# Expert stage of a one-layer MoE trunk: pairs of experts in 64 slots with two gate/up passes, down projection in float32 on raw weights

## The reference

```python
g_val, g_idx = lax.top_k(group_prob, 1)
e_val, e_idx = lax.top_k(in_group, TOP_K_IN_GROUP)            # 2 of the 8 experts of the group
e_w = jax.nn.softmax(e_val, axis=-1) * g_val
for grp in range(N_GROUPS):                                   # 4 groups of 8 experts
    hid = (jax.nn.silu(jnp.einsum('nd,edf->nef', t, w_e_gate[sl]))      # 2048 -> 256
           * jnp.einsum('nd,edf->nef', t, w_e_up[sl]))
    out = out + jnp.einsum('nef,efd->nd', hid * combine[:, sl, None], w_e_down[sl])   # 256 -> 2048
```

## Time and profile before

| | us |
|---|---|
| median of 3 runs | 1174.81 |
| the runs | 1174.03, 1174.81, 6625.89 |
| span of the profiled execution | 1173.3 |

### The profile page before, as it was taken

The page is one execution under the profiler, slowest core; times in us unless marked ns, Lnnn a source line. Parts: engine busy times, 40 slices in busy tenths (PEclk is TensorE's granted clock), DMA queues, the critical chain, the costliest instruction groups (busy, mean ns, idle before and its releaser), DMA issues.

```text
span 1173.3 us, 15718 instructions
## 1 busy us (share of the span) xinstructions
PE 1148.3 (98%) x5398; PEld 952.8 (81%) x5398; DVE 827.2 (70%) x741; ACT 675.1 (58%) x610; POOL 19.5 (2%) x21
## 2 busy tenths in 40 slices
PE   7999999999999999999999999999999999999995
PEld 6888888888888888878878888888888888888884
DVE  5546565565554545654578887988879888798887
ACT  5335555643333344443567776677766777667774
POOL 0000000000000000111100000000000000000000
PEclk8999999999999999999999999999999999999998
DMA  9554444577566565585659998999989999799991
GB/s 314 189 188 162 153 162 174 173 244 271 194 201 211 190 209 177 199 285 178 215 180 333 382 374 306 313 375 379 373 299 319 371 385 373 291 325 368 378 354 74
DMA packets 115094, 312.05 MB, mean 266 GB/s; under 512 B 14152, under 2 KB 15216, under 8 KB 114544
## 3 DMA queue, kind: packets, MB, share of 16 engines
q1 hardware_dynamic: 115056, 311.55, 74.7%
HBM read 309.41 MB, written 2.10 MB: 265 GB/s over the span
## 4 chain that ended last, share of the span: by engine, by line
PE 90%; DVE 5%; ACT 3%; issue 2%; DMA 0%; DVEq 0%; SPq 0%; ACTq 0%
PE bank L1392 28%; PE bank L1394 27%; PE bank L1393 27%; PE bank L1699 2%; ACT whi L528 1%; DVE wlo L1238 1%; DVE o_lo L1278 1%; PE bank L1494 1%; DVE wlo L849 1%; PE bank L1518 1%; PE bank L1686 1%; PE bank L1596 0%; DMA x<-in_x 0%; DVE y_out L1366 0%; DVE xs L873 0%
## 5 line engine op out<-in xcount | busy, mean ns | idle before, releaser
L1238 DVE TENSOR_TENSOR wlo<-xraw,whi 128x2048 fp32r<-128x2048 f32 x186 | 425.1, 2291 | 71.3 <-ACT whi L528 70.2
L528 ACT ACTIVATE whi<-xraw 128x2048 fp32r<-128x2048 f32 x188 | 360.7, 1919 | 94.8 <-PE bank L1394 93.2
L849 DVE TENSOR_TENSOR wlo<-raw,whi 128x2048 fp32r<-128x2048 f32 x92 | 214.8, 2336 | 209.2 <-ACT whi L528 209.2
L528 ACT ACTIVATE whi<-raw 128x2048 fp32r<-128x2048 f32 x92 | 176.2, 1916 | 255.0 <-PE bank L1394 255.0
L1392 PE MATMUL bank<-whi,actT_hi 128*128 128x512 f32 x608 | 240.6, 396 | 4.9 <-DVE actT_lo L880 2.1
L1394 PE MATMUL bank<-wlo,actT_hi 128*128 128x512 f32 x608 | 237.6, 391 | 0.0
L1393 PE MATMUL bank<-whi,actT_lo 128*128 128x512 f32 x608 | 237.4, 390 | 0.0
L1392 PE MATMUL bank<-whi,xg_hi 128*128 128x512 f32 x512 | 202.0, 394 | 0.3 <-DVE wlo L1238 0.3
L1394 PE MATMUL bank<-wlo,xg_hi 128*128 128x512 f32 x512 | 199.6, 390 | 0.0
L1393 PE MATMUL bank<-whi,xg_lo 128*128 128x512 f32 x512 | 199.5, 390 | 0.0
L1392 PEld LDWEIGHTS bank<-whi,actT_hi 128*128 128x128 f32 x608 | 114.6, 188 | 31.4 <-DVE wlo L849 3.7
(11 more groups left out here) (216 smaller groups left out, 861.6 us busy)
## 6 DMA issues: line engine op xcount, KB each, us to landing
xraw<-in_w_e_gate SPq DMA_DIRECT2D x126, 512.0 KB, 5.0
xraw<-in_w_e_up SPq DMA_DIRECT2D x126, 512.0 KB, 6.5
xraw<-in_w_e_down SPq DMA_DIRECT2D x124, 512.0 KB, 6.1
raw<-in_w_gate SPq DMA_DIRECT2D x64, 512.0 KB, 4.3
raw<-in_w_in SPq DMA_DIRECT2D x56, 512.0 KB, 4.6
raw<-in_w_out SPq DMA_DIRECT2D x32, 512.0 KB, 4.8
raw<-in_w_branch_a SPq DMA_DIRECT2D x16, 512.0 KB, 4.7
raw<-in_w_branch_b SPq DMA_DIRECT2D x16, 512.0 KB, 4.7
```

The lines of the kernel that those rows point to most:

```text
L528: return act.activation(whi[slot][:], src, ACT.Copy)
L849: dve.tensor_tensor(wlo[s][:], raw[:, k, :], whi[s][:], ALU.subtract).then_inc(lo_made, 1)
L1238: dve.tensor_tensor(wlo[s][:], place(i, j, q)[0], whi[s][:], ALU.subtract).then_inc(lo_made, 1)
```

## The change

1. **Slots by pair.** A group's 8 experts form 4 pairs. A token is given a slot in each pair in which it has an expert, 64 slots (`CAP`) a pair. `selp` holds these 0/1 matrices. `gather` now multiplies the fp32r parts `hg_hi` and `hg_lo` by the four pairs at once (256 columns) and leaves both parts beside each other in `xe`: 64 slots of high part and 64 of low part form the 128 stationary columns of gate/up.
2. **Gate/up in two passes.** PE multiplies the stacked columns by `whi` and by `wlo`: rows 0 to 63 of the result hold the high part's product, rows 64 to 127 the low part's. ACT copies the lower gate rows (`gate_low`), DVE adds them (`gate_sum`), ACT runs silu for both row halves, and the matmul that turns the hidden rows has the 0/1 matrix `p2` in place of the identity: it adds the two halves and puts each row at its slot among the group's 128.
3. **Down in float32.** `hT_e` is kept in float32, and `down` multiplies it by the loaded weights as they are: no `whi`/`wlo`, one float32 matmul for each 512 columns. There are two `whi`/`wlo` pairs now.
4. **Loads.** Down row blocks come in one DMA of 1 MiB. The order in the queue becomes gate/up 0, 1, down block 0 of the expert before, gate/up 2, 3, down block 1. A place with a down block is free when PE has used it (`after_down`). Before the first group 8 pieces are loaded instead of 10.
5. **Routing.** The counts run over 20 columns (4 groups and 16 pairs) in place of 4, `hg` is made in two parts on DVE (`gained`) instead of on POOL, and tokens for which a pair or group has no room go through all 32 experts in float32, under an `If`.

From the diff, cut to what is spoken of:

```diff
+        def gate_up_at(j, k4):
+            return 2 + k4 if j == 0 else (0, 1, 3, 4)[k4]
+        def down_at(j, f):
+            return (j + 1, (2, 5)[f]) if j + 1 < EPG else (EPG, f)
...
+                if j == 0:
+                    after_down(i - 1, EPG - 2, 0)
+                    load_gate_up(i, 0, 0, e)
+                    after_lo(i - 1, EPG - 1, 2)
+                    load_gate_up(i, 0, 1, e)
+                    after_lo(i - 1, EPG - 1, 3)
+                    load_gate_up(i, 0, 2, e)
+                    after_down(i - 1, EPG - 2, 1)
+                    load_gate_up(i, 0, 3, e)
+                elif j == 1:
+                    if not first:
+                        after_down(i - 1, EPG - 1, 0)
+                        load_gate_up(i, 1, 0, e)
+                        after_down(i - 1, EPG - 1, 1)
+                        load_gate_up(i, 1, 1, e)
+                        after_lo(i, 0, 0)
+                        load_down(i, 0, 0, e)
...
-            pool.wait_ge(g2_in, 16)
-            with pool.Fori(0, NC) as n:
-                for t in range(TT):
...
+            def gained(n):
+                steps = Chain(dve, hg_step, 4 * n)
+                for t in range(TT):
+                    dve.wait_ge(acc_free, 2 * (A1 + A2 + NC) + 2 + 2 * n + t + 1)
+                    cols = bass.ds(n * COLS, COLS)
+                    dve.wait_ge(hg_made, 2 * n + t + 1)
+                    steps.link(dve.tensor_tensor(hgt[:], resid[:, t, cols], gbig[:, cols], ALU.mult))
+                    steps.link(dve.tensor_copy(permuted(hg_hi[t][:], n), by_rows(hgt[:])))
+                    dve.tensor_tensor(permuted(hg_lo[t][:], n), by_rows(hgt[:]), permuted(hg_hi[t][:], n),
+                                      ALU.subtract).then_inc(hg_made, 1)
...
+            def group_v(i, after_another, another_follows):   # DVE
+                if after_another:
+                    output_lo(i - 1)
+                for j in range(EPG):
+                    expert_lo(i, j, 2)
+                    if j == 0:
+                        weights(i)
+                    expert_lo(i, j, 3)
+                    if j == 0 and after_another:
+                        add(i - 1, range(0, 6), SCATTER)
+                    if j < EPG - 1:
+                        expert_lo(i, j + 1, 0)
+                        gate_sum(i, j)
+                        expert_lo(i, j + 1, 1)
+                        hidden(i, j)
+                    if j == 0 and after_another:
+                        add(i - 1, range(6, 8), SCATTER)
...
+            def gate_up(i, j, k4):
+                    for part in (whi, wlo):
+                        mm = pe.matmul(dst[:], x, part[s][:].rearrange("p (u k f) -> p u k f", u=2, k=4)[:, :, k, :],
+                                       start=(kt == 0 and part is whi), stop=(kt == KT - 1 and part is wlo))
...
+            def down(i, j, f, blocks):
+                for b in blocks:
+                    mm = pe.matmul(bank[2 + b][:], hT_e[:, f, :], src[:, b * COLS:(b + 1) * COLS],
+                                   start=(j == 0 and f == 0), stop=last)
...
+            def gather(i, kts):
+                for kt in kts:
+                    if kt > 1:
+                        pe.wait_ge(xe_by_dve if kt % 2 else xe_by_act, KT // 2 * i + kt // 2)
+                    for h, part in enumerate((hg_hi, hg_lo)):
+                        for t in range(TT):
+                            mm = pe.matmul(bank[6 + kt % 2][:, h * 256:(h + 1) * 256], part[t][:, kt * P:(kt + 1) * P],
+                                           selp[:, t, 0:NP, :].rearrange("p r s -> p (r s)"),
...
+                for j in range(1, EPG):                       # PE, one expert
+                    gate_up(i, j, 0)
+                    down(i, j - 2, 1, (2, 3))
+                    turn_hidden(i, j - 1)
+                    gate_up(i, j, 1)
+                    down(i, j - 1, 0, (0, 1))
+                    gate_up(i, j, 2)
+                    down(i, j - 1, 0, (2, 3))
+                    gate_up(i, j, 3)
+                    down(i, j - 1, 1, (0, 1))
+                last = EPG - 1                                # PE, the seam
+                    gather(i + 1, range(0, 2))
+                down(i, last - 1, 1, (2, 3))
+                    gather(i + 1, range(2, 4))
+                turn_hidden(i, last)
+                    gather(i + 1, range(4, 7))
+                down(i, last, 0, (0, 1))
+                    gather(i + 1, range(7, 10))
+                down(i, last, 0, (2, 3))
+                    gather(i + 1, range(10, 13))
+                down(i, last, 1, (0, 1))
+                    gather(i + 1, range(13, 16))
+                down(i, last, 1, (2, 3))
```

More of the change, by code:

```diff
@@ L40 @@
 DENSE_RAW, DENSE_PARTS = 4, 2
-EXP_RAW, EXP_PARTS = 6, 3
+ROW = 6
+CAP = 64
 LOWEST = -3.0e38
@@ new lines, in gate_low, with silu @@
+            def gate_low(i, j):
+                act.wait_ge(gu_used, hi_count(i, j, 3) + 1)
+                act.activation(g_low[:], bank[j % 2][CAP:P, 0:FF], ACT.Copy).then_inc(g_low_made, 1)
+            def silu(i, j):
+                act.wait_ge(cw_made, 3 * i + 3)
+                act.wait_ge(g_sum_made, EPG * i + j + 1)
+                for h in range(2):
+                    rows = slice(h * CAP, (h + 1) * CAP)
+                    act.activation(s_act[rows, :], g_sum[:], ACT.Silu,
+                                   scale=cw[0:CAP, j // 2, EPG:EPG + 1]).then_inc(silu_made, 1)
@@ L820, in _ @@
+            bring_table(ACT.Silu)
+            for kt in range(0, KT, 2):
+                gathered_a(0, kt)
             group_a(0, False, True)
@@ new lines, in _ @@
+            dve.wait_ge(rank_full, 2)
+            for t in range(TT):
+                order.mark(dve.scalar_tensor_tensor(out=pos[:, t, :], in0=bank[2 + t][:, 0:NM], scalar=1.0,
+                                                    in1=member[:, t, :], op0=ALU.add, op1=ALU.mult))
+            order.wait()
+            for t in range(TT):
+                order.mark(dve.tensor_tensor(over[:, t, :], pos[:, t, :], room_of[:], ALU.subtract))
+            order.wait()
+            order.link(dve.tensor_reduce(worst[:], over[:], AX_X, ALU.max))
@@ L1215, in _ @@
+            gathered_v(0, 1)
+            dve.tensor_scalar(left[:], kept[:], -1.0, 1.0, ALU.mult, ALU.add).then_inc(left_made, 1)
             dve.wait_ge(gexp_made, TT)
@@ new lines, in group_v @@
+                if another_follows:
+                    expert_lo(i + 1, 0, 0)
+                gate_sum(i, EPG - 1)
+                if another_follows:
+                    gathered_v(i + 1, 1)
+                hidden(i, EPG - 1)
+                if another_follows:
+                    gathered_v(i + 1, 3)
+                    expert_lo(i + 1, 0, 1)
+                    for kt in range(5, KT, 2):
+                        gathered_v(i + 1, kt)
+                else:
+                    output_lo(i)
@@ L1665, in down @@
-            def down(i, j, start, stop):
-                pe.wait_ge(hT_lo_made, EPG * i + j)
-                for f in range(2):
-                    m = 6 * j + 2 + f
-                    q = 4 + f if not stop else f
-                    if stop:
-                        m = 6 * j - 2 + f
-                    s = (4 + q) % EXP_PARTS
-                    pe.wait_ge(lo_made, DENSE_RAW + DENSE + PER_G * i + m + 1)
-                    for b in range(4):
-                        cols = slice(b * COLS, (b + 1) * COLS)
-                        mm = three(bank[2 + b][:], hT_hi[:, f, :], hT_lo[:, f, :], whi[s][:, cols], wlo[s][:, cols],
-                                   start and f == 0, stop and f == 1)
-                        if stop and f == 1 and b < 3:
-                            mm.then_inc(o_full, 1)
-                    mm.then_inc(piece_used, 1)
+            pe.wait_ge(e_lo, 1)
```

801 lines of the change are left out of this document (417 added, 384 removed).

## The result

The changed kernel takes **1262.5 us** (median of 4 runs, 1261.4 to 1263.7) against 1174.8 for the kernel before: ratio 1.075, 95% interval 1.074 to 1.076. It is slower, and outside the range that was predicted (1160 to 1218). One run of the kernel before took 6625.9 us; it stands outside the comparison, and its cause is not known. The profiled execution has a span of 1260.5 us, 71.3 more than the 1189.2 of my sum. The direction came as forecast: the loads took over from PE. The size did not, and what sets their pace is not what I had priced.

A forecast was written before the change was run, and what follows sets the result against it. PE paced the kernel before; the load queue was to take over. The first group's last gate/up at 716.7, three periods of 147.7 and the tail gave 1189.2, with 1.5 for the median 1191 us; range 1160 to 1218.

The forecast's parts named there:

- my sum: Whole kernel: the forecast's terms added up to a span of 1189.2 us, against 1173.3 before.
- The ring's length: Inside a group, from one landing of gate/up piece 0 through PE's down half to the next: 15.65 us, pace taken 15.5.
- 0.2 + 2.5 + 5.1: Inside a group, from the down block's release to the next piece 0's landing: hand-over 0.2, fixed 2.5, transfers 5.1 us.
- the runs of loads: Inside groups, 30 pieces and then three times 33, up to the last gate/up's end: 86.2 us and 94.0 us each.
- The queue stays at its 40 us rate: Rival, loads inside groups: 2.75 us a piece, 16.5 an expert, total 1212 us; chance 0.24.
- bounds of the pace are 15.36 and 15.65: Inside a group, time per expert: between the queue's 15.36 us and the walked 15.65; 15.5 taken.
- The loads keep PE's pace: Rival, loads inside groups: 14.7 us an expert, needing 428 GB/s, total 1174 us; chance 0.17.
- PE's terms: PE's work per expert: 14.70 us against 16.58, with float32 matmuls of 512 columns at 0.875 and the turn at 0.45.
- The seam: Between two groups, from the old group's last gate/up to the next group's first down block done: 53.7 us.
- Routing: Before the first group: gather starts at 588.2 and takes 10.2 us, first gate/up at 598.4, 10.8 later than before.
- up to 4 us: In the routing, idle PE falling to the lower clock slows the 24 idle matmuls: up to 4 us more, not summed.
- The sign of the whole: Whole kernel: slower by 15.9 us, the saving per expert being spent at the seam, three times.

The follow-up runs named there:

- experiment 1: Changed kernel with SP's load list reordered, each down block asked for one gate/up piece later except a group's last: 1203.6 us.
- experiment 5: Changed kernel with the down blocks asked for by POOL on a DMA queue of their own, gate/up loads in their old order on SP: 1208.1 us.
- experiment 3: Changed kernel with only the second down block (f = 1) of each expert asked for later, f = 0 left in place: 1258.4 us.
- experiment 9: Kernel with reordered list, moved rounding and moved additions (1177.7 us), loading only 1 KiB of each 8 KiB row in all down blocks but the first: 1163.2 us.
- version two: Kernel with reordered list, moved rounding and moved additions (1177.7 us), last gained rows after the second last logits, 36 idle matmuls for 24: 1174.5 us.

## Why the prediction was wrong

**The ring's length: the step that failed.** I walked the right ring, "The next piece 0 so lands at t+7.85+0.2+2.5+5.1 = t+15.65", and made 15.5 an expert of it. The turn shown above takes 17.8. The term that was mis-sized is 0.2 + 2.5 + 5.1 = 7.8 us from the release of the down block to the landing: it measures 9.5 in that turn (650.78 to 660.28), 10.2 in the turn of the timelines (838.88 to 849.08), and 8.3 to 10.8, on the mean 9.5, in the 21 such waits that the chain shows. The 2.5 + 5.1 is the landing in an empty queue. I had only one ring in mind; the block f = 0 with pieces 2 and 3 makes a second one, half an expert away, whose last piece is still in the queue: in the timelines it is taken at 842.79, 3.7 us after the bunch of f = 1 was asked for. A small term was low too: gate/up 2.08 and not 1.81. This step holds most of the 58 us that the runs of loads are longer by (some turns have the lower clock as well), and with the list reordered 59 us come back. That the order of waits in SP's list makes the rings is shown by experiments 1 and 5, and that one ring is enough to keep the pace by experiment 3; that the rest of the other bunch is what delays the landing is read from the timelines, and was not tried by itself.

**The rivals.** "The queue stays at its 40 us rate" ended on the right side, at 1212, for a reason that was not the cause: the queue could go faster (412), it was not asked. No rival had a ring longer than the queue's pace; "bounds of the pace are 15.36 and 15.65" left no room above. "The loads keep PE's pace" needed 428 GB/s: with the rings broken, the best 20 us stretches reach 416 to 419 (794 to 814 of experiment 1) and the best 40 us 415, and experiment 9 puts a price of 14.5 us on what is missing, so the earlier trace rows with their 412 were the better guide. The Trainium skill ("DMA: Bandwidth & Descriptors", Bandwidth) has a long load at 425; no stretch of 20 us that I read in these runs shows it.

**PE's terms held.** A float32 matmul of 512 columns costs 0.865 (1.73 for two, each with two records) against 0.875 forecast; the turn 0.45; an expert of PE alone 14.7 to 14.8 against 14.70 (experiment 9).

**The seam: 56.6 to 58.8 for 53.7.** The gather was mis-sized: a 256-column matmul takes 0.19 (four in 0.75), not 0.12, and nine blocks of four make 2.4 us of it; each needs new weights, whose load alone takes 0.23:
```profile
L1769 PEld LDWEIGHTS bank<-selp,hg_hi 128*128 128x128 f32 x96 | 18.5, 227 | 28.4 <-issue 11.4 <-ACT xe L797 9.3 <-DVE xe L1314 7.3
```
ACT's wait for the first piece lasted to T0+6.2 and not 4.1 in the first seam, and to T0+4.5 and 4.6 in the others. PE's pauses brought the lower clock, which I had priced nowhere in the seam: eight gate/up matmuls took 3.78 us in place of 1.86.
```profile
946.00:950.00 4.00, 1.80 (x4) 1.49 (x5) 4.00 (x3) 1.64 (x3) 0.00 (x0) 0.67 0.56 203
950.00:954.00 4.00, 4.00 (x12) 3.16 (x11) 2.04 (x4) 1.91 (x1) 0.00 (x0) 0.50 0.94 328
```
PE had been idle for 3.8 us before these, waiting for a split behind six additions.

**Routing: first gate/up at 601.4 for 598.4.** The gather started 1.3 us later than forecast and took 12.0 us instead of 10.2. PE was idle from 570.10 to 574.40, and the granted clock from 572 to 580 was 0.50: the 16 logits matmuls took 3.63 us, twice the 1.87 of the same line at 560.89, and the 24 idle ones 7.51 for 5.4, which held the counts 1 us (asked for from 584.3, begun at 585.5). The Trainium skill ("TensorE: Matmul & The Clock Gate", Part 1: The HAM clock gate) says that an engine that was idle falls back to its lower clock, and the trace agrees: 0.50 after 4.3 us of idle. I had weighed this with up to 4 us and left it out of the sum.

**The sign of the whole.** The change saves PE 1.8 us an expert (16.58 against 14.8), 14 a group, and the seam takes 8.6 of it: 138.9 a group where PE alone counts, against 144.5 before. The queue (14.5 us by experiment 9) and the later start (first gate/up at 597.4 even in version two, against 587.6) take the rest, so even the mended kernel only ties with the one before.

## To carry to other kernels

A DMA list that is issued in order is part of every ring that passes through it: for each wait in it, write down the loads that stand behind, and fill a place that comes free late only after the places that are free already. Count all rings that share the queue, and take the landing with the others' loads ahead of it, since the landing in an empty queue is the shortest there is. A DMA share near 1 is no proof of the limit; reorder or leave out bytes before believing it.

## What the runs showed of the hardware

- Loads of the same sizes moved at 357 to 370 GB/s over 40 us when asked for in bunches behind a wait, and at up to 415 with the list reordered. From 840 to 860 it was 371 at a DMA share of 0.99 against 412 at 1.03.
- In bunches that share the queue with those of the other ring, the first gate/up piece behind a down block landed 8.3 to 10.8 us after the block's release, where the empty queue had let me expect 7.8.
- Loads of 1 MiB in rows of 8 KiB were no slower than two of 512 KiB in rows of 4 KiB; the split kernels took 9 and 13 us more for 64 blocks.
- A matmul of 256 columns with new weights each time takes 0.19 us, far more than half of the 0.2267 of 512 columns; its weight load alone takes 0.23.
- A float32 matmul of 512 columns takes 0.865 us in two records.
- After 4.3 us of idle PE in the routing, and 3.8 before the split at a seam, the granted clock was 0.50, the lower of its two levels (1.2 of 2.4 GHz), and the same matmuls took twice their time.
